# Neighbourhood attention by blocks of 8 by 16 queries, with a bias table and scores two units ahead

## What is computed

```python
def row_block(r):                      # kh = 8 rows, kw = 16 columns
    rs = jnp.clip(r - kh // 2, 0, rows - kh)
    kr = lax.dynamic_slice_in_dim(kg, rs, kh, axis=1)
    kwin = kr[:, :, key_cols]          # key_cols = clip(col - 8, 0, 48) + 0..15
    bias = rpb[:, drow[None, :, None], dcol[:, None, :]]
    s_loc = einsum('bwhd,biwjhd->bhwij', qr, kwin) * ATTN_SCALE + bias
    s_ctx = einsum('bwhd,bchd->bhwc', qr, kc) * ATTN_SCALE
    p = softmax(concatenate([s_loc, s_ctx]))
    return p_loc @ vwin + p_ctx @ vc
```

## Time and profile before

| | |
|---|---|
| median of 3 runs | 1372.49 us (1371.92 to 1376.0) |
| the profiled execution: its time | 1372.62 us |
| its span | 1370.7 us |
| TensorE busy | 1329.0 us (97%) |
| VectorE busy | 994.3 us (73%) |
| ScalarE busy | 686.8 us (50%) |
| GpSimd busy | 235.3 us (17%) |
| mean granted TensorE clock | 0.997 |

### The profile page before, as it was taken

The page is one execution under the profiler, slowest core; times in us unless marked ns, Lnnn a source line. Parts: engine busy times, 40 slices in busy tenths (PEclk is TensorE's granted clock), DMA queues, the critical chain, the costliest instruction groups (busy, mean ns, idle before and its releaser), DMA issues.

```text
span 1370.7 us, 24028 instructions
## 1 busy us (share of the span) xinstructions
PE 1329.0 (97%) x8352; PEld 733.4 (54%) x8352; DVE 994.3 (73%) x1601; ACT 686.8 (50%) x1308; POOL 235.3 (17%) x165
## 2 busy tenths in 40 slices
PE   7999999999988999999899999999999999999997
PEld 1565665445666777777545544444444444444443
DVE  3879885777888999999345697666666666666387
ACT  2532134445777888888322654444444445312225
POOL 0000000332514900000000123233333330000001
PEclk9999999999999999999999999999999999999999
DMA  9637601241400300300011222222222223898953
GB/s 375 221 134 284 212 31 62 83 117 32 113 0 10 115 31 0 92 0 1 16 46 46 78 76 82 81 77 77 69 81 72 77 68 108 271 340 280 353 184 138
DMA packets 118154, 155.35 MB, mean 113 GB/s; under 512 B 17356, under 2 KB 79052, under 8 KB 116812
## 3 DMA queue, kind: packets, MB, share of 16 engines
q1 hardware_dynamic: 113104, 152.03, 32.9%
q10 hardware_dynamic: 4988, 2.50, 0.6%
HBM read 132.09 MB, written 22.42 MB: 113 GB/s over the span
## 4 chain that ended last, share of the span: by engine, by line
PE 58%; DVE 7%; issue 4%; DMA 3%; ACT 3%; ACTq 0%; POOL 0%; POOLq 0%; DVEq 0%; SPq 0%
PE PS L980 51%; PE PS L1277 7%; DMA arena<-in_w_ffn_out 3%; ACT arena L1706 1%; DVE arena L2642 1%; DVE arena L2645 1%; DMA arena<-weight_sum_rows 1%; DVE arena L2406 1%; DVE arena L2522 1%; PE PS L1047 1%; ACT arena L1924 1%; DVE arena L2512 0%; ACT arena L1696 0%; DVE arena L2570 0%; DVE arena L2555 0%
## 5 line engine op out<-in xcount | busy, mean ns | idle before, releaser
L980 PE MATMUL PS<-arena 128*128 128x512 f16 (+6 forms) x7048 | 1207.8, 330 | 20.9 <-DMA arena<-in_w_mod 7.0
L980 PEld LDWEIGHTS PS<-arena 128*128 128x128 f16 (+3 forms) x7048 | 604.8, 102 | 559.6 <-issue 39.9
L2406 DVE SCALAR_TENSOR_TENSOR arena<-arena 128x512 f16<-128x512 f32 x148 | 120.7, 822 | 76.6 <-ACT arena L1767 76.6
L1767 ACT ACTIVATE arena<-arena 128x512 f16<-128x512 f32 x140 | 87.5, 629 | 130.4 <-PE PS L980 130.4
L1706 ACT ACTIVATE arena<-PS 128x512 f16<-128x512 f32 (+2 forms) x256 | 118.6, 531 | 51.5 <-PE PS L1277 51.5
L2342 DVE SCALAR_TENSOR_TENSOR arena<-PS,arena 128x512 f16<-128x512 f32 (+2 forms) x256 | 140.0, 599 | 4.6 <-ACT arena L1706 2.5
L1277 PE MATMUL PS<-arena 128*128 128x128 f32 x864 | 115.7, 280 | 6.5 <-ACT arena L1696 6.1
L1696 ACT ACTIVATE arena<-PS,arena 128x1280 f32<-128x1280 f32 (+1 forms) x96 | 118.0, 1230 | 1.1
L1277 PEld LDWEIGHTS PS<-arena 128*128 128x128 f32 x864 | 93.8, 141 | 44.1 <-ACT arena L1696 43.2
L1879 ACT ACTIVATE arena<-arena 128x512 f16<-128x512 f32 x77 | 48.2, 629 | 129.0 <-DVE arena L2555 71.7
L2334 DVE TENSOR_REDUCE arena<-PS 128x1 f32<-128x1280 f32 x64 | 95.5, 1492 | 22.9 <-PE PS L980 22.9
(11 more groups left out here) (180 smaller groups left out, 1061.7 us busy)
## 6 DMA issues: line engine op xcount, KB each, us to landing
arena<-in_w_ffn_out SPq DMA_DIRECT2D x121, 256.0 KB, 4.8
arena<-in_w_mod SPq DMA_DIRECT2D x24, 1024.0 KB, 7.3
arena<-in_w_ffn_in SPq DMA_DIRECT2D x88, 256.0 KB, 2.9
arena<-in_w_in SPq DMA_DIRECT2D x9, 1024.0 KB, 5.6
left_operands<-arena SPq DMA_DIRECT2D x33, 256.0 KB, 2.2
arena<-left_operands SPq DMA_DIRECT2D x3, 2816.0 KB, 15.3
arena<-in_x SPq DMA_DIRECT2D x2, 2048.0 KB, 12.9
arena<-cst_fwd SPq DMA_DIRECT2D x4, 1024.0 KB, 11.4
```

The lines of the kernel that those rows point to most:

```text
L980: return pe.matmul(out, lhsT, rhs, start=start, stop=stop, skip_group_check=True)
L1767: act.activation(aS[n % RING][:, 0], weight_block(p, b), ACT.Copy, scale=WS).then_inc(blk_hi, 1)
L2406: dve.scalar_tensor_tensor(dst[:, 1], src, WS, dst[:, 0], ALU.mult, ALU.subtract).then_inc(blk_lo, 1)
```

## The change

The queries of a unit become a block of 8 grid rows by 16 columns (`j // 4` picks the half of the grid, `j % 4` the columns). All its neighbours lie in 12 rows by 32 columns, 384 keys, so a unit has 640 columns: three tiles of near keys and two of context. Queries are put into block order when they are copied out of PSUM; near keys are read from the key tensor with a step; the values of each of the four column windows are gathered by 16 DMAs into `nearV`. The bias with its mask comes as a table from DRAM, 384 columns for six kinds of block, one load a head; everything that made it on the chip is gone. P is turned into the third bank of its parity and the upper half of the output bank, so scores wait only for the exponentials of the unit two before, and they and the maximum are issued two units ahead. The outputs of the blocks are in block order; transposes of the mixed outputs are regrouped into twelve groups of four, of which those of the near part write back to token order, and four groups are issued around the last value matmuls.

```diff
+Q_COLS, K_ROWS, K_COLS, N_NEAR = 16, 12, 32, 384
+KEY_COL = (0, 8, 24, 32)
...
+    out["lay_bias"] = np.ascontiguousarray(rpb[:, neighbours()].reshape(HN, P, 6 * N_NEAR), np.float32)
...
-        self.banks = [range(0, 4), range(4, 7)] if self.na else [range(0, 4), range(4, 8), range(8, 10)]
+        self.banks = [range(0, 3), range(3, 5)] if self.na else [range(0, 4), range(4, 8), range(8, 10)]
...
-        if bank == 2:
+        if bank == len(self.banks) - 1:
             return 512 * (6 + self.par) + 256
-        return 1536 * self.par + 512 * (bank + (self.na and bank == 1))
+        return 1536 * self.par + (1024 if self.na else 512 * bank)
...
+        nearV = [f16(o, 4, HN, 2, HD) for o in (20, 24, 32, 36)]
+        bias = [f32(40, 6, N_NEAR), f32(52, 6, N_NEAR)]
...
+        MIX_TURNS = ([("near", 0), ("near", 1)] + [("mix", t) for t in range(4)] + [("near", 2), ("near", 3)]
+                     + [("mix", t) for t in range(4, NT)])
...
+            def load_near(cw):
+                for r in range(4):
+                    p = GRID_W * (r % 2) + KEY_COL[cw]
+                    rows = V[p:p + K_COLS, 0:NT, HKV:HKV + HN].rearrange("p (g e) h a d -> p g e (h a d)", e=2)
+                    sp.dma_start(nearV[cw][K_COLS * r:K_COLS * r + K_COLS].rearrange("p g h a d -> p g (h a d)"),
+                                 rows[:, :, r // 2]).then_inc(near_in[cw // 3], 16)
+            def load_late(n):
+                g, kp = n // 4 + 2, n % 4
+                load(chunk_index("late", n), w_mod[:, 2 * kp:2 * kp + 2, GW * g:GW * g + GW], (2, GW))
             sp.wait_ge(split_lo, n_split(chunk_index("qkv", 5)))
-            for h in range(HN):
-                if h >= 2:
-                    sp.wait_ge(bias_rdy, 5 * (h - 1))
-                for a in range(2):
-                    src = bass.AP(tensor=skew, offset=(h * 19 + 1 - a) * 64 * P + 63,
-                                  ap=[[P - 1, 64], [64 * P, 18], [1, GRID_W]])
-                    sp.dma_start(J[64 * a:64 * a + 64, h % 2], src).then_inc(J_in[h % 2], 16)
...
+            sp.wait_ge(pr_vl, n_valued(GROUP0[0] - 1))
+            for cw in range(3):
+                load_near(cw)
+            load_late(12)
+            load_late(13)
+            sp.wait_ge(pr_mm, GROUP0[1])
+            load_near(3)
+            sp.dma_start(flat(bias[0]), lay["bias"][0]).then_inc(bias_in[0], 16)
+            load_late(14)
+            load_late(15)
+            sp.wait_ge(late_rdy, 4)
+            for n in range(2):
+                t0 = (16, 40)[n]
+                sp.dma_start(gates[n].rearrange("(t p) -> p t", p=P), mod[:, t0:t0 + 8, 0],
+                             allow_slow_non_contiguous=True).then_inc(gates_out, 16)
+            sp.wait_ge(gates_out, 32)
+            sp.wait_ge(pr_mm, NU)
+            sp.dma_start(flat(bias[1]), lay["bias"][1]).then_inc(bias_in[1], 16)
+            sp.wait_ge(pr_tc, NU)
+            sp.dma_start(gate1, gates[0].partition_broadcast(P)).then_inc(gates_in, 16)
+            for n in range(2):
+                load(chunk_index("wo", n), w_out[:, 0:4, 512 * n:512 * n + 512], (4, 512))
+            for h in range(2, HN):
+                sp.wait_ge(bias_add, NT * (h - 1))
+                sp.dma_start(flat(bias[h % 2]), lay["bias"][h]).then_inc(bias_in[h % 2], 16)
...
-            def column_mask(h):
-                pool.wait_ge(J_in[h % 2], 32 * (h // 2 + 1))
-                own.step(pool.tensor_tensor(J[:, h % 2], J[:, h % 2],
-                                            cmask.unsqueeze(1).broadcast_to((P, 18, GRID_W)), ALU.add))
-            def bias_of(h, kind):
-                o = bias_shift(kind)
-                pool.tensor_tensor(bias[:, h % 2, kind], J[:, h % 2, o:o + 10],
-                                   rmask[:, kind, :].unsqueeze(2).broadcast_to((P, 10, GRID_W)), ALU.add)\
-                    .then_inc(bias_rdy, 1)
...
                     q, k = nqT[:, u.blk, u.j * P:u.j * P + P], nkT[:, u.blk]
-                    k0 = window(u.j) * P
-                    pieces = ((512, 128, k0 + 512), (640, 256, S), (0, 512, k0))
+                    o, half, col = 1536 * u.par, u.j // 4, KEY_COL[u.j % 4]
+                    if u.v >= 2:
+                        pe.wait_ge(s_exp, u.n - 1)
+                    for part in range(2):
+                        near = k[:, part, 0:S].rearrange("p (r c) -> p r c", c=GRID_W)
+                        mm(PSf[:, o:o + N_NEAR].rearrange("p (r c) -> p r c", c=K_COLS), q,
+                           near[:, 4 * half:4 * half + K_ROWS, col:col + K_COLS], part == 0, False)
+                    for part in range(2):
+                        mm(PSf[:, o + N_NEAR:o + 512], q, k[:, part, S:S + P], False, part == 1)
+                    for part in range(2):
+                        ins = mm(PSf[:, o + 512:o + 640], q, k[:, part, S + P:S + C], part == 0, part == 1)
                 else:
                     q, k = qT[:, u.j, tok(u.blk)], kT[:, u.kv]
-                    pieces = ((1024, 256, 1024), (0, 512, 0), (512, 512, 512))
...
+                    for o, w, s0 in ((1024, 256, 1024), (0, 512, 0), (512, 512, 512)):
+                        before = u.ahead(-2)
+                        if before.na and o == 1024:
+                            copied(before, 0)
+                        elif not before.na and o < 1024:
+                            copied(before, o // 512)
...
                 ins.then_inc(s_mm, 1)
...
-                    if u.na and b == 1 and u.v >= 2:
-                        copied(u.ahead(-2), 1)
-                    if b == 2:
+                    if u.na and b == 0 and u.v >= 2:
+                        copied(u.ahead(-2), 0)
+                    if b == len(u.banks) - 1 and u.v >= 2:
                         pe.wait_ge(o_rdy, u.n - 1)
                     for i in bank:
...
-                tiles = [window(u.j) + i for i in range(5)] + [NT, NT + 1] if u.na else range(10)
-                for i, kt in enumerate(tiles):
-                    if i == 0 and not u.na:
-                        copied(u, 2)
-                    elif i % 4 == 0 and u.na:
-                        copied(u, i // 4)
-                    first, last = i == 0, i == len(tiles) - 1
+                copied(u, len(u.banks) - 1)
+                n = 5 if u.na else 10
+                for i in range(n):
+                    first, last = i == 0, i == n - 1
                     if u.na:
+                        v = nearV[u.j % 4][:, u.j // 4 + i, u.blk] if i < 3 else V[:, NT + i - 3, HKV + u.blk]
                         for part, vp in ((0, 0), (1, 0), (0, 1)):
-                            ins = mm(PS[:, 6 + u.par, 0:HD], PT[:, u.par, part, i], V[:, kt, HKV + u.blk, vp],
+                            ins = mm(PS[:, 6 + u.par, 0:HD], PT[:, u.par, part, i], v[:, vp],
...
             def attend(u):
-                if u.v < NV - 1:
+                if NNA - 1 <= u.v < NV - 1:
                     scores(u.ahead(1))
                 turn_p(u)
+                if u.v < NNA - 2:
+                    scores(u.ahead(2))
                 if u.v:
                     weigh(u.ahead(-1))
...
             turn_p(Unit(0))
             turn_qk(NU - 1)
-            pe.wait_ge(pr_tc, NU - 1)
+            scores(Unit(2))
+            pe.wait_ge(pr_tc, NU)
+            for n in range(2):
+                pe.wait_ge(near_in[n], 16 * (12, 4)[n])
             attend(Unit(1))
-            pe.wait_ge(pr_tc, NU)
             attend(Unit(2))
...
+            def turn_mix(i):
+                what, n = MIX_TURNS[i]
+                if what == "mix":
+                    pe.wait_ge(oab_sum, n + 1)
+                if i >= 6:
+                    pe.wait_ge(mx_lo, i - 3)
+                for k in range(4):
+                    ps = PS[:, mix_bank(i)]
+                    if what == "mix":
+                        ins = pe.transpose(ps[:, k * P:k * P + P], mixtok[:, n, k * P:k * P + P], ident)
+                    else:
+                        f = 4 + n % 2
+                        ins = pe.transpose(ps.rearrange("p (r b c) -> p b r c", b=4, c=Q_COLS)[:, k],
+                                           mixtok[:, 4 * (n // 2) + k, f * P:f * P + P],
+                                           ident.rearrange("p (r c) -> p r c", c=Q_COLS))
+                ins.then_inc(mx_mm, 1)
             for v in range(89, NV):
                 attend(Unit(v))
+            turn_mix(0)
+            turn_mix(1)
+            turn_mix(2)
             weigh(Unit(NV - 1))
...
+            turn_mix(3)
...
-                        ins = act.copy(nqT[:, :, tok(t)], ps[:, 4:8])
+                        for r in range(2):
+                            q = 2 * t + r
+                            o = S // 2 * (q // 8) + Q_COLS * (q % 8)
+                            dst = nqT.rearrange("p h (g b t) -> p h g b t", g=2, b=4)[:, :, q // 8, :,
+                                                                                    o % P:o % P + Q_COLS]
```

(18 more changed lines are left out.)

182 lines of the change are left out of this document (63 added, 119 removed).

## The result

| | before | changed |
|---|---|---|
| median of 4 runs, us | 1372.65 (1371.92 to 1376.0) | 1352.66 (1349.17 to 1354.15) |
| ratio, 95% interval | | 0.9846 (0.9821 to 0.9871) |
| profiled execution (span), us | 1372.6 (1370.7) | 1349.17 (1347.4) |

A forecast was written before the change was run, and what follows sets the result against it. The neighbourhood stage was taken as bound by a ring of waits among TensorE, VectorE and ScalarE, none full. Savings of 22.2 (stage), 1.0 (GpSimd's mask) and 2.3 (mix transposes) make 25.5: 1372.6 - 25.5 = 1347 us, range 1340 to 1358.

The forecast's parts named there:

- the ring: Neighbourhood stage: TensorE, VectorE and ScalarE wait for one another in turn; 3.015 us a unit before, 2.2 computed after.
- narrow-ring rival: Neighbourhood stage: scores two units ahead buy nothing, only the width pays; 2.55 us a unit, 1354.4 us in all; chance 0.17.
- The stage: Neighbourhood stage, from unit 1's turns of P to unit 32's: 72.8 us for 95.0, so 22.2 us less.
- VectorE's 2.09: Neighbourhood stage: VectorE's own time a unit, 2.09 us after the narrowing, from 2.63.
- TensorE's 1.68 us: Neighbourhood stage: TensorE's matmuls a unit, turns 0.59, fifteen value matmuls 0.56 and scores 0.53, 1.68 us.
- The allowance of 0.1 us a unit: Neighbourhood stage: added to 2.2 us for loop ends and collisions among nearly full engines, giving 2.3 us a unit.
- The last two units: End of the neighbourhood stage, turns of unit 30 to unit 32: 6.1 us, 7.6 before.
- GpSimd's mask: Before the neighbourhood stage: removing GpSimd's mask, which holds up a VectorE instruction, saves 1.0 us (bounds 0 and 1.05).
- The mix transposes: End of the attention: twelve transposes ahead of the last value matmuls fill TensorE's idle times, saving 2.3 us.
- The late table: Neighbourhood stage: head 1's bias table lands late behind other loads, VectorE waits 12 us; 1359 us; chance 0.08.
- Strided operands: Score matmuls and mix transposes: short runs of columns slow TensorE, up to 4.6 us plus 2 us; 1353.6 us; chance 0.05.
- The clock: Neighbourhood stage: TensorE's clock falls to 1.2 GHz, 3.6 us a unit, ending slower at 1386 us; chance 0.04.

The follow-up runs named there:

- a_handover: The changed kernel with unit 31 turned and its low halves taken before the scores and maximum of unit 32; median 1353.55 us.
- b_no_mask: The kernel before without GpSimd's first column mask (head 0); median 1371.46 us, ratio 0.9999.
- a_mix_late: The changed kernel with all mix transposes behind the last weighing and the wait for the last scaled output; median 1353.84 us.
- a_one_ahead: The changed kernel with scores and maximum one unit ahead and exponentials behind the copies, as in the kernel before; median 1354.92 us.
- a_plain_keys: The changed kernel with TensorE's neighbourhood loop written out and near keys read side by side (other keys than the right ones); median 1343.72 us.
- b_unroll_pe: The kernel before with TensorE's loop over the heads of the neighbourhood stage written out; median 1372.67 us.

## Why the prediction was right, and where its steps were off

The sign and the ring were right, and the time is in the range; the sum was 25.5, the profiled executions differ by 23.3, the medians by 20.0. The time alone doesn't confirm the mechanism: the narrow-ring rival's 1354.4 us is nearer to the median of 1352.66 than the forecast's 1347. The mechanism rests on the traces.

**The stage (22.2 counted, 18.7 measured).** ScalarE's 1.95 us a unit and the new ring of 2.2 hold: with TensorE's addresses fixed, the period is 2.10. VectorE's 2.09 is a little high: from the start of its reduce to the end of its reciprocal it takes 1.95, because the low half now starts together with the read-out of the sum. It is busy for 1.85 of them, so "over 88% busy" would have failed at the forecast's own period of 2.3 as well. The step that was mis-sized is TensorE's 1.68 us, "fifteen 0.56". It was taken from unit 30 of the kernel before, a unit that stands outside the loop. Inside it the changed kernel's 21 matmuls of a unit take up to 2.29 us, and over the loop's 24 units the kernel loses 7.6 to 8.0 us against fixed addresses. The allowance of 0.1 us a unit "for loop ends and collisions" hid part of this by luck: 2.3 forecast, 2.38 measured. (0.4 of the 18.7 us is the low clock in the trace of the kernel before.) "No engine can force more than 2.1 us" was wrong: TensorE's instruction stream did.

**The last two units (6.1 counted, 7.3 measured).** "The scores of 32 and 33 begin after the first low half" overlooked that the lead of two units must be given back there. All of it lies from unit 30 to 31, 4.0 us for the 2.85 counted and 2.9 one ahead; from 31 to 32 both take 3.3. a_handover shows that exchanging the order only moves the wait.

**GpSimd's mask (1.0).** 1.2 measured by b_no_mask. The 1.1 between the starts of unit 1 in the two traces is only by chance so near to it: from the 24 matmuls on the changed kernel gains 1.7, mask and low clock together, and at those matmuls it is 0.6 late (288.15 for 287.58), as it is already at 265 us, ahead of the gathers. The loads cost nothing, as said: the gathers leave SP's queue from 271.72, and no wait for the bias tables shows.

**The mix transposes (2.3).** 2.2 measured, their place shown to be the cause by a_mix_late.

**The rivals.** *The narrow ring only* is refuted as a description (a_one_ahead is slower), but close in size: 2.51 us a unit, 2.49 from unit 5 on, and with the cheaper end of the stage it lies 2.8 us above the changed kernel. The late table did not occur; head 1's load left at 345.96 as forecast, the four tables landed after 5.8 to 10.1 us, 6.9 in the median, and VectorE never waited for one:

```profile
arena<-lay_bias SPq DMA_DIRECT2D x4, 1152.0 KB, 6.9
```

*Strided operands* cost nothing, for keys (a_plain_keys) and for transposes (a_mix_late); what the Trainium skill's page "SBUF — State Buffer", section "Door 1: The DMA port swizzle (why `[64,N]` ≈ `[32,N]`)", says of non-contiguous patterns in PSUM, that they significantly slow matmuls, is not borne out for these runs of 16 columns. *The clock*: the granted clock stayed at 1.00 from 350 us to the end of the stage.

**What is left.** Behind the attention, 1.2 us were gained that no term claims. From the turns of unit 32 to the end of the span are 928.2 us in the changed kernel and 927.8 to 930.1 in the eight others that are alike from there on; the 931.7 of before, less the 2.2 of the mix transposes, are 929.5. The same programs scatter by more: b_no_mask has 933.2 and b_unroll_pe 936.5 where before has 931.7. So the 1.2 us are scatter, not the change's. And the changed kernel's profiled execution is the fastest of its four, 3.5 us under their median. Where such differences arise can be seen in two traces whose programs are the same up to the stage, the changed kernel's and a_handover's, from 300 to 340 us:

```profile
300.00:340.00 40.00, 37.54 (x256) 22.27 (x255) 26.89 (x87) 20.61 (x64) 5.84 (x8) 1.00 0.16 50
```

```profile
300.00:340.00 40.00, 39.15 (x242) 23.07 (x240) 24.61 (x76) 18.86 (x58) 4.77 (x7) 0.91 0.16 47
```

The granted clock is 1.00 in the first and 0.91 in the second, so part of it ran at 1.2 GHz, and TensorE's first turns of P start at 339.76 and at 342.38 us. Such a dip lies somewhere between 300 and 350 us in eleven of the fourteen traces, and in three (the changed kernel's, a_mix_late's and b_no_mask's) it is missing. Why the one dips and the other doesn't, with TensorE doing the same work ahead of it, stays open.

## What to carry to other kernels

Take the duration of an instruction from the loop in which it will run, not from a copy of it outside: short matmuls with an address from a register can be held back by their own instruction stream, and an engine that looks 93% busy may be issuing, not computing. When a ring is shortened, ask first what each engine's stream allows; here the order two units ahead was worth 2.2 us over 25 units with the loop, and 7.5 with it written out. Before two traces are subtracted, compare the granted clock of the stretch in both. A lead that a stage builds up is paid back where the next stage cannot keep it.
